# A decoder step for a prompt and eight sequences: the residual stream held feature-major, feed-forward unrolled in pairs

## The chip, the cores and the metric

One core of a Trainium2 chip runs the whole program. The metric is the device time of one execution in microseconds; the median of several runs is compared. In the profile the engines are PE (TensorE, with PEld for its weight loads), DVE (VectorE), ACT (ScalarE), POOL (GpSimd) and SP (SyncE, which here issues the transfers).

## The reference

One layer of a hybrid decoder is computed for 1024 prompt tokens and for 8 sequences of 4 new tokens: T = 1056 tokens in all, of D = 1024 features, which KD = 8 chunks of 128 partitions hold. All is fp32. Cut to what matters:

```python
def _rmsnorm(x, g):
    return x * rsqrt(mean(x * x, axis=-1) + NORM_EPS) * g

h = _rmsnorm(x, g_mix) @ w_in                     # split into u, v, q, k/v rows, gates
a_out = _gmlp_mixer(u, v)                         # causal gating in chunks of 128
b_out = nsa(q, ...)                               # compressed, selected and window branches, gated
x = x + concat(_rmsnorm(a_out, g_a), _rmsnorm(b_out, g_b)) @ w_o
mk, mv = _rmsnorm(mem, g_mem) @ w_mk, ... @ w_mv  # 256 memory tokens of the prompt
x = x + cross_attend(_rmsnorm(x, g_xa) @ w_xq, mk, mv) @ w_xo
a, g = h @ w_up, h @ w_gate                       # h = _rmsnorm(x, g_ffn), D_FF = 2816
x = x + (gelu(conv3(a) + conv_b) * g) @ w_down
y = _rmsnorm(x, g_final)
```

The samples take their past from a paged cache (gathered by a page table), from a window cache and from a cache of memory keys and values.

## The kernel before, in words

The program is a row of blocks, each with one hand-written stream for each engine, semaphores between the streams and a barrier at its end. A semaphore that an instruction waits for is named in the code (`pe.wait_ge(done, n)`). SP issues the loads in the order in which its stream has them, and a wait in that stream holds back all loads behind it.

*Layouts.* The residual stream `K.X` lies token-major: nine tiles of 128 tokens on the partitions (the last has the 32 sample rows), 1024 features in a row. Matmuls contract over the partitions, so what goes into a product as the normed input lies feature-major, `K.HT`: 8 chunks of 128 features, T = 1056 columns. A full fp32 product runs in two passes, and the trace has two records for it. In the feed-forward each operand is split into a high and a low part of type fp32r, and three products (high by high, high by low, low by high) take the place of the fp32 one.

*Norm of a tile* (`norm_phase`, and inside `project_norm`): ACT squares a row of 1024 with a running sum (L122), ACT takes the root (L127 or L343), DVE inverts and scales (L134, L141, L146), PE transposes the eight 128 x 128 blocks (L176, L298: a "turn"), DVE copies the result out times the gain (L156).

*The stages in order of time.* `norm_phase` "mix" with the bias rows (L1252, six small products of the relative bias table beside it); `feature_major` for w_in (L235: ring of two weight chunks, pieces of 352 columns, 8 chunks by 3 pieces by 8 products) while SP gathers pages of the cache (L460); gating (L538); compression; the samples' attention; the prompt's attention (L1080 to L1103); `project_norm` "wo" (L317, `w_o` as the moving operand in halves of 512 columns, token tile stationary, the norms of the two halves of the mix ahead of it and the next norm behind it, all by turns); norm "mem"; `feature_major` for w_mk; `memory_values` (L1286); `feature_major` for w_xq; cross attention of prompt and samples; `project_norm` "xo", which also splits its result into `ff_in_high` (ACT) and `ff_in_low` (POOL); `ffn`.

*The samples' attention* works on four sequences at a time ("half" 0 and 1). A sequence's 32 query rows are 32 stationary columns, so the four write the four groups of 32 partitions of one bank. `score(half)` has one sequence after the other: two products of 512 keys of the gathered pages (L862), two of 32 new keys (L863, L864), 512 window keys (L865), 63 compressed keys (L866). PV (L901) has 15 blocks for each sequence, again one sequence after the other. Score(1) reads the pages that SP gathers anew once score(0) has released them.

*`ffn`* goes over 22 chunks of 128 hidden features. For each, up and gate (L1654) are 3 pieces of 352 by 8 by 3 products each. Five turns of a hardware loop hold four chunks and then their part of down (L1667): four quarters of 256 output features, nine token tiles, activations stationary, w_down moving. Weights come by SP to `ff_weights` and `ff_down`, ACT makes the high part (L1684, L1690), POOL the low part (L1605, L1609). DVE does the convolution (L1762 to L1774) and adds the down products to x (L1785). Two chunks and the rest of down follow behind the loop, and the final norm by tiles (ACT L1734, DVE L1792).

## Time and profile before

| what | us |
|---|---|
| runs before, median of 3 (lowest, highest) | 2360.38 (2358.34, 2360.42) |
| the profiled execution | 2355.33 |
| its span | 2353.5 |
| PE busy | 2177.7 (93%), 11612 instructions |
| PEld busy | 1687.5 (72%) |
| DVE busy | 755.6 (32%) |
| ACT busy | 546.3 (23%) |
| POOL busy | 243.8 (10%) |

The span runs from the first to the last instruction of the profiled execution; its own time is 1.83 us more. Busy time overlaps between engines, and PEld lies beside PE. The page's line on transfers has 145.62 MB moved, mean 62 GB/s.

### The profile page before, as it was taken

To read this page: it belongs to the slowest core of one execution; us is meant where nothing else is said; L and a number is where in the kernel's file an instruction comes from. 1 tells how busy PE (TensorE), PEld (TensorE's weight loads), DVE (VectorE), ACT (ScalarE), POOL (GpSimd) and SP (SyncE) were. 2 spreads that over 40 slices of the span, in tenths; PEclk is the share of its full clock that TensorE was granted. 3 is DMA by queue.
4 is the path that set the end of the run, shared out by engine and by line. 5 is a ranking of instruction groups with operands and counts; after the bars stand their busy time and mean duration, and the time that the engine had idled before them with its cause. 6 is when DMAs were issued, how large, how long until landed. Compare 5 with 4: busy or idle time off the path is not lost. (4 is left out here: it accounts for less than half of the span.)

```text
span 2353.5 us, 29783 instructions
## 1 busy us (share of the span) xinstructions
PE 2177.7 (93%) x11612; PEld 1687.5 (72%) x11612; DVE 755.6 (32%) x1767; ACT 546.3 (23%) x1293; POOL 243.8 (10%) x122
## 2 busy tenths in 40 slices
PE   7989989679999997998997889899999999999997
PEld 4655557357677774546566634399999999999996
DVE  2002240335455453320003212235244342443425
ACT  3013220025455553211002101222021120211203
POOL 0000000000000000000000001223123231232311
PEclk9999999879899998999999999999999999999998
DMA  7230036330010002004102420011111010110102
GB/s 250 77 118 2 1 96 184 99 121 23 23 45 22 22 0 107 0 1 161 45 27 108 161 108 1 20 47 55 37 54 55 19 63 28 54 55 21 62 14 91
DMA packets 89308, 145.62 MB, mean 62 GB/s; under 512 B 41005, under 2 KB 63597, under 8 KB 86925
## 3 DMA queue, kind: packets, MB, share of 16 engines
q1 hardware_dynamic: 85118, 140.95, 17.9%
q10 hardware_dynamic: 4088, 3.17, 0.5%
q8 instruction: 82, 1.34, 0.2%
q14 instruction: 20, 0.16, 0.0%
HBM read 132.95 MB, written 14.26 MB: 63 GB/s over the span
## 5 line engine op out<-in xcount | busy, mean ns | idle before, releaser
L1654 PE MATMUL ps<-ff_in_high,ff_weights_high 128*128 128x352 f32 x1056 | 342.8, 325 | 13.2 <-issue 6.9
L1654 PE MATMUL ps<-ff_in_low,ff_weights_high 128*128 128x352 f32 x1056 | 340.1, 322 | 0.0
L1654 PE MATMUL ps<-ff_in_high,ff_weights_low 128*128 128x352 f32 x1056 | 339.9, 322 | 0.0
L317 PE MATMUL ps<-big 128*128 128x512 f32 (+1 forms) x576 | 252.9, 598 | 1.3 <-PEq L1449 1.3
L1667 PE MATMUL ps<-ff_down_high,ff_act_high 128*128 128x256 f32 x792 | 228.8, 289 | 9.4 <-POOL ff_act_low L1614 5.2
L235 PE MATMUL ps<-big,top 128*128 128x352 f32 x768 | 229.4, 462 | 2.9 <-ACTq L242 2.9
L1667 PE MATMUL ps<-ff_down_low,ff_act_high 128*128 128x256 f32 x792 | 226.1, 286 | 0.0
L1667 PE MATMUL ps<-ff_down_high,ff_act_low 128*128 128x256 f32 x792 | 226.0, 285 | 0.0
L1654 PEld LDWEIGHTS ps<-ff_in_high,ff_weights_high 128*128 128x128 f32 x1056 | 199.5, 189 | 14.1 <-issue 7.7
L235 PEld LDWEIGHTS ps<-big,top 128*128 128x128 f32 x768 | 146.6, 191 | 85.9 <-ACTq L242 4.2
L317 PEld LDWEIGHTS ps<-big 128*128 128x128 f32 (+1 forms) x576 | 104.2, 183 | 137.9 <-issue 137.7
L1654 PEld LDWEIGHTS ps<-ff_in_low,ff_weights_high 128*128 128x128 f32 x1056 | 199.8, 189 | 0.0
L1654 PEld LDWEIGHTS ps<-ff_in_high,ff_weights_low 128*128 128x128 f32 x1056 | 199.2, 189 | 0.0
L1103 PE MATMUL ps<-top,big 128*128 128x128 f32 (+1 forms) x1184 | 166.7, 289 | 13.2 <-ACT big L1205 7.2
L1103 PEld LDWEIGHTS ps<-top,big 128*128 128x128 f32 (+1 forms) x1184 | 145.6, 194 | 32.2 <-ACT big L1205 15.4
L538 PE MATMUL ps<-big 128*128 128x512 f32 (+3 forms) x432 | 160.5, 533 | 6.6 <-DVE top L571 6.6
L1667 PEld LDWEIGHTS ps<-ff_down_high,ff_act_high 128*128 128x128 f32 x792 | 153.8, 194 | 12.2 <-DVE x L1785 6.6
L1667 PEld LDWEIGHTS ps<-ff_down_low,ff_act_high 128*128 128x128 f32 x792 | 154.1, 195 | 0.0
L1667 PEld LDWEIGHTS ps<-ff_down_high,ff_act_low 128*128 128x128 f32 x792 | 154.0, 195 | 0.0
L1785 DVE TENSOR_TENSOR x<-ps,x 128x256 f32<-128x256 f32 (+1 forms) x216 | 91.1, 423 | 191.9 <-PE ps L1667 190.3
L538 PEld LDWEIGHTS ps<-big 128*128 128x128 f32 (+1 forms) x432 | 78.6, 183 | 87.5 <-issue 80.2
L1605 POOL TENSOR_TENSOR ff_weights_low<-ff_weights,ff_weights_high 128x1024 fp32r<-128x1024 f32 x44 | 105.6, 2400 | 308.8 <-ACT ff_weights_high L1684 308.8
(273 smaller groups left out, 2545.4 us busy)
## 6 DMA issues: line engine op xcount, KB each, us to landing
ff_weights<-in_w_up SPq DMA_DIRECT2D x22, 512.0 KB, 3.6
ff_weights<-in_w_gate SPq DMA_DIRECT2D x22, 512.0 KB, 4.1
ff_down<-in_w_down SPq DMA_DIRECT2D x20, 512.0 KB, 3.8
x<-in_x_prompt SPq DMA_DIRECT2D x16, 512.0 KB, 9.3
big<-bias_rows SPq DMA_DIRECT2D x8, 960.0 KB, 4.6
top<-in_mem_kt SPq DMA_DIRECT2D x7, 1024.0 KB, 11.0
big<-in_w_tm SPq DMA_DIRECT2D x8, 652.0 KB, 17.4
top<-in_mem_v SPq DMA_DIRECT2D x5, 1024.0 KB, 17.3
```

Of the source, the lines that this page charges most:

```text
L235: last = nc.tensor.matmul(K.bank[3 * u + s][:, 0:b - a], ring[:, u, k, :], src[:, k, a:b], start=k == 0, stop=k == KD - 1)
L317: last = nc.tensor.matmul(K.bank[2 * (t % 2) + h][:r, :], src[:, k, t * P:t * P + r], w[:, h, k, :], start=k == 0, stop=k == KD - 1)
L538: last = nc.tensor.matmul(K.bank[3 * (t % 2) + s][:r, 0:b - a], K.HT[:, k, t * P:t * P + r], w[:, k, a:b], start=k == 0, stop=k == KD - 1)
L1103: last = nc.tensor.matmul(K.bank[7][:, 0:P], pt[u % 2][:w, first + x, :], v, start=first + x == 0, stop=end and x == len(bl) - 1)
L1605: nc.gpsimd.tensor_tensor(w_low[:, s], landing[:, s], w_high[:, s], ALU.subtract).then_inc(low_done[s], 1)
L1654: last = nc.tensor.matmul(K.bank[3 * s + x][:, 0:b - a], w[:, s, k, :], h[:, k, a:b], start=k + n == 0, stop=k == KD - 1 and n == 2)
L1667: last = nc.tensor.matmul(K.bank[6 + n % 2][:, 0:256], a[:, k, t * P:(t + 1) * P], w[:, q % 2, k, :], start=k + m == 0, stop=k == chunks - ...
L1785: nc.vector.tensor_tensor(x, K.bank[6 + n % 2][:rows_of(t), 0:256], x, ALU.add).then_inc(down_taken, 1)
```

## The change

*Residual stream.* `K.XT` holds x as 8 chunks of 128 features by 1056 tokens. The input comes so from memory (`xt`, three pieces of 352 tokens for all features, `PIECES`), the output goes so, and the memory tokens too (`mem_t`). A new class `FeatureNorm` norms a piece: ACT squares two halves of four chunks, DVE adds up the chunks (three additions: 8 to 4, 4 to 2, 2 to 1), one product with a matrix of ones sums over partitions and spreads the sum to all of them (`spread`, L123), ACT takes the root, DVE inverts and multiplies eight chunks by gain and inverse. In the input phase there is no adding up: the product with ones runs over all eight chunks.

*Blocks.* `input_phase` takes the place of the constants' block, `norm_phase` "mix" and `feature_major`; the bias products (L272) stand between the chunks of that product. `mix_output` takes the place of `project_norm` "wo", norm "mem", and the products of w_mk, w_mv and w_xq. `cross_output` takes the place of `project_norm` "xo". In both, w_o and w_xo are stationary, 8 output chunks by 3 pieces by 8 products of 352 columns.

*Samples.* Score and PV have the kind (or block) as the outer loop and the sequence as the inner one.

*Feed-forward.* No hardware loop. Down runs for each pair of chunks: w_down stationary, 3 pieces by 8 output chunks by 6 products of 352 columns. The last pair's weights use the places of the up and gate weights. The final norm goes by pieces; POOL multiplies pieces 0 and 1 by the inverse, DVE piece 2.

```diff
+class FeatureNorm:
...
+    def add_up(self, dve, p):
+        a, b = self.pieces[p]
+        sq = self.sq[p % len(self.sq)]
+        dve.wait_ge(self.squared, 2 * p + 2)
+        for i in range(self.adds):
+            w = KD >> (i + 1)
...
+            add = self.nc.vector.tensor_tensor(sq[:, 0:w, 0:b - a], sq[:, 0:w, 0:b - a], sq[:, w:2 * w, 0:b - a], ALU.add)
...
+    def spread(self, pe, p):
...
+        n = KD >> self.adds
+        for c in range(n):
+            last = self.nc.tensor.matmul(self.bank[:, 0:b - a], self.K.ones[:, :], self.sq[p % len(self.sq)][:, c, 0:b - a],
+                                         start=c == 0, stop=c == n - 1)
+        last.then_inc(self.total, 1)
...
+def input_phase(nc, K, I, O):
...
+            for p, (a, b) in enumerate(PIECES):
+                sp.dma_start(K.XT[:, :, a:b], I["xt"][:, :, a:b]).then_inc(x_came[p], 16)
...
+            weights(2)
+            sp.wait_ge(norm.scaled, 3)
+            sp.wait_ge(came, 48)
+            gather(sp, K, 0, "cmp", 0, 2)
+            weights(3)
+            gather(sp, K, 0, "cmp", 2, 2)
...
-                for n in range(4):
-                    s = 4 * half + n
-                    rows = slice(32 * n, 32 * n + 32)
-                    for i in range(2):
-                        nc.tensor.matmul(K.bank[i][rows, :], qbd[:, s, :], KS[:, n * 1024 + 512 * i:n * 1024 + 512 * i + 512], start=True, stop=True)
...
+                for kind in range(6):
+                    for n in range(4):
+                        s = 4 * half + n
...
-                for n in range(4):
-                    s = 4 * half + n
-                    rows = slice(32 * n, 32 * n + 32)
-                    for i, (x, w) in enumerate(blocks):
+                for i, (x, w) in enumerate(blocks):
+                    for n in range(4):
+                        s = 4 * half + n
+                        rows = slice(32 * n, 32 * n + 32)
...
+def mix_output(nc, K, I, O, memt, mkt, mv):
...
+            sp.wait_ge(wo_done, n_wo)
+            for h in range(2):
+                sp.dma_start(w_mv[:, h], I["w_mv"][h]).then_inc(mv_came[h], 16)
+            for c in range(2, KD):
+                sp.wait_ge(mk_done, c - 1)
+                sp.dma_start(mk_ring[:, c % 2], I["w_mk"][c]).then_inc(mk_came[c % 2], 16)
...
+                    for k in range(KD):
+                        last = nc.tensor.matmul(K.bank[n % 4][:, 0:b - a], w[:, c, k, :], K.HT[:, k, a:b],
+                                                start=k == 0, stop=k == KD - 1)
+                    last.then_inc(wo_done, 1)
+                    if p < 2 and c in (1, 3, 5):
+                        turn(3 * p + 3 + c // 2)
...
+def cross_output(nc, K, I, w, w_came, high, low, sq, root, first_chunk):
...
+                norm.root(act, p)
+                act.wait_ge(norm.scaled, p + 1)
+                for h in range(2):
+                    nc.scalar.activation(high[:, 4 * h:4 * h + 4, a:b], sq[:, 4 * h:4 * h + 4, 0:b - a], ACT.Copy).then_inc(high_made, 1)
...
+            def down(g):
+                pe.wait_ge(act_low, 2 * g + 2)
+                pe.wait_ge(d_low_made, 2 * g + 2)
+                for p, (a, b) in enumerate(PIECES):
+                    for o in range(KD):
+                        n = g * TILE + p * KD + o
+                        if n >= 2:
+                            pe.wait_ge(down_taken, n - 1)
...
+                            for m, (w, x) in enumerate(((dh, a_high), (dl, a_high), (dh, a_low))):
+                                last = nc.tensor.matmul(K.bank[6 + n % 2][:, 0:b - a], w[:, at], x[:, c % SLOTS, a:b],
+                                                        start=e + m == 0, stop=e == 1 and m == 2)
...
+            up_and_gate(0)
+            up_and_gate(1)
+            for g in range(PAIRS - 1):
+                up_and_gate(2 * g + 2)
+                if g == PAIRS - 2:
+                    up_and_gate(2 * g + 3)
+                down(g)
+                if g < PAIRS - 2:
+                    up_and_gate(2 * g + 3)
+            down(PAIRS - 1)
+            norm.spread(pe, 2)
```

How the change moves instructions is shown at three places. The first is TensorE's order in `score(0)` of the samples, before (these five rows stand there four times, once for each sequence):

```order
L862 MATMUL ps<-x,big 32x512 x2
L863 MATMUL ps<-top,big 32x32
L864 MATMUL ps<-top,big 32x32
L865 MATMUL ps<-top,big 32x512
L866 MATMUL ps<-top,big 32x63
```

And with the change (the first row behind the scores is a transpose of the probabilities' first block):

```order
L697 MATMUL ps<-top,big 32x63 x4
L697 MATMUL ps<-top,big 32x32 x8
L697 MATMUL ps<-x,big 32x512 x8
L697 MATMUL ps<-top,big 32x512 x4
L706 MATMUL ps<-ident,big 63x128
```

The same 24 products stand in groups of one kind, and in each group four neighbours write four different groups of 32 rows of the bank.

The second is SP's order from the load of w_o to that of w_xq, before:

```order
L259 DMA big<-in_w_o 128x4096 x2
L1964 DMA top<-in_mem_prompt 128x1024 x2
L203 DMA top<-in_w_mk 128x1024 x2
L284 UNCONDITIONAL_BRANCH
L100 UNCONDITIONAL_BRANCH
L259 DMA big<-in_w_mv 128x4096 x2
L99 UNCONDITIONAL_BRANCH
L215 UNCONDITIONAL_BRANCH
L203 DMA top<-in_w_mk 128x1024 x6
L214 UNCONDITIONAL_BRANCH
L1272 UNCONDITIONAL_BRANCH
L203 DMA top<-in_w_xq 128x1024 x2
```

And with the change:

```order
L1083 DMA big<-in_w_o 128x1024 x8
L1084 DMA top<-in_mem_t 128x2048
L1086 DMA top<-in_w_mk 128x1024 x2
L1088 DMA top<-in_w_xq 128x1024 x2
L1091 DMA big<-in_w_mv 128x4096 x2
L1094 DMA top<-in_w_mk 128x1024 x6
L1096 DMA out_mem_k<-top 128x2048
L1098 DMA out_mem_v<-top 128x2x1024
L1102 DMA top<-in_w_xq 128x1024 x6
```

The two loads of w_mv still stand ahead of the last six of w_mk, but no memory norm lies between the end of w_o, which they wait for, and the products of w_mk. The first two chunks of w_xq have moved ahead of both.

The third is TensorE's order in the product of w_xo. Before it goes by token tiles, a turn of the tile before behind each:

```order
L317 MATMUL ps<-big 128x512 x32
L298 MATMUL ps<-ident,ff_scaled 128x128 x8
L317 MATMUL ps<-big 128x512 x16
L298 MATMUL ps<-ident,ff_scaled 128x128 x8
L317 MATMUL ps<-big 128x512 x16
```

And with the change, up to the block's end (`ones` is the matrix of ones, `ff_squares` the added squares of a piece):

```order
L1277 UNCONDITIONAL_BRANCH
L1287 MATMUL ps<-big 128x352 x96
L123 MATMUL ps<-ff_squares,ones 128x352
L1287 MATMUL ps<-big 128x352 x64
L123 MATMUL ps<-ff_squares,ones 128x352
L1287 MATMUL ps<-big 128x352 x32
L123 MATMUL ps<-ff_squares,ones 128x352
L1272 UNCONDITIONAL_BRANCH
```

Nine turns have become three single products; the last of them stands behind all products of the block.

## Rows read from the trace of the kernel before

**Rows 1.** Stretches: start:end, length; busy (count) of PE, PEld, DVE, ACT, POOL; PEclk, DMA, GB/s
```profile
0.00:33.11 33.11, 15.88 (x84) 9.84 (x85) 16.78 (x31) 16.89 (x29) 0.40 (x6) 1.00 0.87 326
33.11:148.70 115.59, 115.55 (x384) 73.76 (x384) 0.00 (x0) 8.23 (x21) 0.00 (x0) 0.99 0.29 78
415.97:424.63 8.66, 8.61 (x48) 2.86 (x48) 0.01 (x1) 0.00 (x0) 0.00 (x0) 1.00 1.03 252
442.28:451.10 8.82, 8.82 (x59) 3.69 (x59) 2.47 (x6) 0.00 (x0) 0.00 (x0) 0.97 0.00 0
481.02:497.40 16.38, 16.33 (x120) 12.59 (x120) 0.01 (x1) 0.00 (x0) 0.00 (x0) 0.92 0.00 1
918.68:1059.60 140.92, 138.70 (x417) 65.44 (x416) 44.10 (x87) 20.79 (x53) 0.00 (x0) 0.99 0.04 16
1059.60:1069.10 9.50, 3.57 (x17) 3.28 (x17) 4.78 (x10) 2.59 (x5) 0.00 (x0) 0.64 0.84 329
1069.10:1099.20 30.10, 28.68 (x128) 23.90 (x128) 0.00 (x0) 2.68 (x7) 0.00 (x0) 1.00 0.43 140
1129.56:1243.40 113.84, 113.84 (x384) 72.88 (x384) 0.00 (x0) 8.23 (x21) 0.00 (x0) 1.00 0.11 36
1384.89:1526.87 141.98, 133.47 (x361) 59.94 (x361) 30.77 (x54) 25.11 (x48) 25.07 (x20) 0.97 0.04 11
1526.87:2332.25 805.38, 792.41 (x5498) 790.19 (x5499) 313.79 (x493) 140.30 (x199) 213.91 (x93) 0.99 0.14 43
2332.25:2353.50 21.25, 10.45 (x48) 8.77 (x47) 15.53 (x27) 14.18 (x28) 0.00 (x0) 0.62 0.53 204
```

**Rows 2.** The chain that ended last, in the feed-forward: start, us, engine, what
```profile
1646.96 49.21 PE ps L1667 x408
1696.17 1.61 issue
1697.78 68.96 PE ps L1654 x432
...
2281.20 22.91 PE ps L1654 x144
...
2309.26 23.00 PE ps L1667 x168
```

**Rows 3.** Groups of instructions: xcount | busy, mean ns | idle before
```profile
L1605 POOL TENSOR_TENSOR ff_weights_low<-ff_weights,ff_weights_high 128x1024 fp32r<-128x1024 f32 x44 | 105.6, 2400 | 308.8 <-ACT ff_weights_high L1684 308.8
L1764 DVE SCALAR_TENSOR_TENSOR ff_conv<-ff_row,ff_small,ff_conv 128x1024 f32<-128x1024 f32 x22 | 28.3, 1284 | 0.8
L1252 PE MATMUL ps<-top,table 33*8 33x512 f32 (+1 forms) x12 | 5.7, 555 | 0.0
```

**Rows 4.** Timeline of PE in score(0): start, us, engine, line, operation
```profile
417.84 0.60 PE L865 MATMUL ps<-top,big 128*32 128x512 f32 x1
417.85 0.62 PE L862 MATMUL ps<-x,big 128*32 128x512 f32 x1
418.27 0.59 PE L865 MATMUL ps<-top,big 128*32 128x512 f32 x1
```

**Rows 5.** Timeline of DVE behind the first PV
```profile
465.05 0.29 DVE L927 COPY big<-ps 128x128 f32<-128x128 f32 x1 [10.21 <-PE ps L901]
```

**Rows 6.** Timeline of SP's queue, gather of the second half's pages
```profile
425.34 13.34 SPq L460 DMA_DIRECT2D big<-in_pool_sel  x16
```

**Rows 7.** DMA issues of 425 to 445: xcount, KB each, us from issue to landing
```profile
big<-in_pool_sel SPq DMA_DIRECT2D x16, 128.0 KB, 2.6
```

**Rows 8.** DMA issues of 1055 to 1100
```profile
big<-in_w_mv SPq DMA_DIRECT2D x2, 2048.0 KB, 9.6
```

**Rows 9.** Timeline of ACT, a square in the first norm
```profile
9.20 1.03 ACT L122 ACTIVATE ps<-x 128x1024 f32<-128x1024 f32 x1
```

**Rows 10.** Timeline of DVE and POOL in the feed-forward
```profile
2073.53 2.85 POOL L1609 TENSOR_TENSOR ff_down_low<-ff_down,ff_down_high 128x1024 fp32r<-128x1024 f32 x1
2074.04 2.37 DVE L1763 TENSOR_SCALAR ff_conv<-ff_row,ff_small 128x32 f32<-128x32 f32 x1
```

More of the change, by code:

```diff
@@ L129, in _, with square @@
-            if extra and "scalar" in extra:
-                extra["scalar"](act)
+            def square(p):
+                act.wait_ge(x_came[p], 16)
+                for h in range(2):
+                    norm.square(act, p, h)
+            square(0)
+            square(1)
+            act.wait_ge(eps_set, 1)
+            norm.root(act, 0)
+            square(2)
+            norm.root(act, 1)
+            norm.root(act, 2)
+            for n, (c, p) in enumerate(tiles):
+                a, b = PIECES[p]
+                act.wait_ge(done, n + 1)
+                nc.scalar.activation(K.FM[:, c, a:b], K.bank[3 * (c % 2) + p][:, 0:b - a], ACT.Copy).then_inc(taken, 1)
+                if c >= 2 and p == 2:
+                    x, y = cuts[c - 2]
+                    act.wait_ge(product, c - 1)
+                    nc.scalar.activation(vec[:, x:y], K.bank[7][:H, 0:y - x], ACT.Copy).then_inc(rows, 1)
@@ new lines, in _ @@
+            pe.wait_ge(ones_set, 1)
+            for p in range(3):
+                norm.spread(pe, p)
+            for n, (c, p) in enumerate(tiles):
+                a, b = PIECES[p]
+                if c < 2:
+                    pe.wait_ge(norm.scaled, p + 1)
+                else:
+                    pe.wait_ge(taken, nth[c - 2, p] + 1)
+                if p == 0:
+                    pe.wait_ge(w_came[c % 2], 16 * (c // 2 + 1))
+                for k in range(KD):
+                    last = nc.tensor.matmul(K.bank[3 * (c % 2) + p][:, 0:b - a], ring[:, c % 2, k, :], K.HT[:, k, a:b],
+                                            start=k == 0, stop=k == KD - 1)
+                last.then_inc(done, 1)
+                if c >= 2 and p == 2:
+                    x, y = cuts[c - 2]
+                    if c == 2:
+                        pe.wait_ge(came, 48)
+                    else:
+                        pe.wait_ge(rows, c - 2)
+                    nc.tensor.matmul(K.bank[7][:H, 0:y - x], K.table[:, :], oh[:, x:y], start=True, stop=True).then_inc(product, 1)
@@ new lines, in _ @@
+                nc.scalar.activation(a_high[:, c % SLOTS], ct, ACT.Copy).then_inc(act_split, 1)
+            for p, (a, b) in enumerate(PIECES):
+                for h in range(2):
+                    act.wait_ge(down_taken, LAST + KD * p + 4 * h + 4)
+                    norm.square(act, p, h)
+                act.wait_ge(norm.squared, 2 * p + 2)
+                for c in range(KD if p < 2 else TAIL, KD) if p == 2 else range(KD):
+                    last = nc.scalar.activation(K.XT[:, c, a:b], K.XT[:, c, a:b], ACT.Copy, scale=K.gains[:, 5, c:c + 1])
+                    if p == 2 and c == KD - 1 or p < 2 and c % 4 == 3:
+                        last.then_inc(gained, 1)
+                norm.root(act, p, free=(y, 2))
```

1132 lines of the change are left out of this document (525 added, 607 removed).

## The prediction

> **What bounds the kernel now.** I read the table of stretches first [rows 1]: TensorE is busy for all but a few tenths or a few microseconds of nearly every stretch, at a granted clock near 1.00. So the kernel is bound by TensorE's time in matmuls, and what the change can win is columns streamed, stretches in which small products could share the array, and the seams where TensorE stops. Then I read the chain of the feed-forward [rows 2]: it alternates 432 up and gate products (68.96 us, 0.1596 each) with 408 down products of 256 columns (49.21 us, 0.1206 each), and a return of the loop on TensorE of 1.6 to 1.8 us each time. Next came the mean durations of what will stand in the new seams [rows 3, 9], the TensorE timeline of the sample scores, and what surrounds them [rows 4 to 7]. The profiled execution took 2355.33 us, 1.83 more than its span and 5.05 less than the median of the runs (2360.38); I make the sum against the span and add both at the end. A measurement tells about 0.2% (4.7 us) of this kernel from no change.
>
> Two unit prices carry the sum. An fp32 product of 352 columns takes 113.84/192 = 0.593 us (two records each, [rows 1], the 1129.56 row). One of 512 columns is 0.863: the 918.68 row has 138.7 us busy in 417 records; 288 of them are 144 products, the others 16 turns (the eight transposes of a tile) of 0.9, which leaves 124.2.
>
> **The change part by part** (minus is faster).
>
> *Feed-forward, −42.4.* Before, 805.4 us = 22 chunks x 22.95 (68.96/3 and 22.91, [rows 2]) = 504.9; 2328 down products x 0.1206 = 280.8; five loop returns 8.5; a wait of 5.2 for the last activation, 2304.1 to 2309.3; 2.7 because the last 168 down products took 0.1369 instead of 0.1206; 3.3 start. After: down uses w_down as the stationary operand over 352 columns, 11 pairs x 144 products of the up form = 11 x 22.95, so 33 x 22.95 = 757.4, plus start 3.3 and 2.3 at the tail's edge: 763.0. Down alone goes from 2376 products (286.5 us, 48 of them in the tail's row) to 252.5: nine token tiles of 128 for 1056 tokens were 8% padding, which is 24 of these 34 us, and 352 columns cost 0.453 ns each for 0.471. The rest is the loop's seams and the last wait, which now has a whole down pair over it. A two-bank turn of down needs the DVE addition, 0.5 us, to come back in 0.96, so no stall; cost on SP, ACT, POOL stays hidden: they do the same splits, and the busiest of the splitting engines, POOL, has 213.9 of 805 [rows 1], 66 operations of 2.4 and 22 activations. If that cover fails, POOL's last difference of a chunk is late next, at 2.4 us a time, 53 over 22 chunks.
>
> *Sample attention, −26.* Four sequences write four column groups of 32. Score 0 takes 8.66 now; kinds outermost it is three groups of four 512-column products at 0.86 plus the small ones: 2.9. Score 1 then waits for the page gather: SP issues it from 425.34 for 13.34, landing 2.6 later, 441.3 [rows 6, 7], against 442.28 now, so only 1.0 comes of that. Score 1, 8.82, becomes about 4.6. VectorE's idle of 10.21 ahead of 465.05 was the first half's PV [rows 5], 16 us on TensorE like the second. With 1.0 from the gather, 4.2 from score 1 and 10.2 from this PV, what follows moves from 465.05 to about 449.7, −15.4. The second PV, 16.4 in 120 records, goes to 5.9: a quarter would be 4.1, strict order of records 8.2 to 9, and I take a little under the middle; −10.5. Together −26; −29 without lead times, −17 if pairs of records don't pack.
>
> The rows for this are the timeline's three [rows 4]: each fp32 product is two records. L862 of the next sequence starts at 417.85, beside the first record of L865 (417.84) and ahead of its second (418.27). So a product of another column group starts before the earlier one's second record, and four in a row should pack. The Trainium skill, in "TensorE: Matmul & The Clock Gate", section Part 3: Packing small matmuls — row/col tiling, says that matmuls are monotone in start and end in program order. By that rule this term would be −17 (rival 2); the trace speaks against applying it to the records of one product.
>
> *w_o to w_xq, −23.8.* The products: 192 x 0.593 = 113.9 for 124.2. Six turns of 0.93 remain inside the stretch (ten fewer, since the second norm is now a product with ones) = 5.6, and three spreads 1.5: 121.0 for 140.9, −19.9. Three turns ahead of the first product instead of two: +2.2. The memory norm's own block, 9.5 us with TensorE busy 3.57, disappears beside w_o: −9.5. w_mk: 28.7 of products, 0.6 of a spread, and a stall. SP issues both 2 MB halves of w_mv when w_o ends, ahead of w_mk's third chunk. The halves land after 9.6 in the median [rows 8], the second near 11, and 0.5 MB behind it at 329 GB/s is 13; it is needed at 7.3 (two chunks of 3.6), so 5.7, with 1.0 of start: +5.9 on 30.1. Ends: 0 if the queues interleave the loads, 10 if later chunks pay too. w_mv loses the block seam of 30.4 less 32 x 0.863: −2.5. w_xq is unchanged.
>
> *w_xo to the first feed-forward product, −3.6.* Before 142.0. After 113.9 + 1.2 of two spreads, then a tail that nothing covers: the last piece's addition 0.9, square of four rows 1.4 by [rows 9] (1.03 per 1024), additions 3.2, spread 1.2, root and reciprocal 1.0, eight scales 3.6 (1.284/1024 x 352 each, [rows 3]), high part 1.4, two POOL differences 6.6 (2.4/1024 x 1408 each), barrier 0.4, first weights 1.06 + 2.4: 23.3. Sum 138.4. Here the trace of before has no such tail; its bounds are −6 (high and low overlapped by halves) and +3 (VectorE stopped by POOL).
>
> *Input and feature-major product, +1.0.* The constants block goes, and x comes as three pieces of 1.44 MB; at 326 GB/s they land near 7, 11 and 15, squares 2.9 a piece, and the first product starts near 27 for 33.11: −6. Six bias products of 0.95 ([rows 3], 12 records) move from TensorE's idle time into the bound stretch: +5.5. SP's gathers stand between w_fm chunks, one of them late: +1.5. Bounds −5 and +6.
>
> *Final norm, −4.0.* 21.25 becomes 17.2: add 0.9, square 1.4, additions, spread and root 5.5, eight scales 3.6, output 3.0, and 2.8 for VectorE held by POOL's multiply of an earlier piece. The row for it: a 32-column VectorE operation took 2.37 us beside a POOL operation of 2.85 [rows 10], and 2.8 is taken for one such block. The Trainium skill, "SBUF — State Buffer", section Summary: rules for kernel authors, says that a VectorE operation with two SBUF inputs blocks fully until GpSimd's finishes; by that the tail would be 17.2, without it 14.4, and the trace agrees.
>
> *Cross attention, 0*: same instructions. **Sum**: −42.4 −26.0 −23.8 −3.6 +1.0 −4.0 = −98.8. Span 2254.7, profiled execution 2256.5, median of the runs 2261.5.
>
> **The rivals.**
> 1. *The forecast*, chance 0.60, 2261.5.
> 2. *Records start strictly in order.* A product's two records share a column group and follow each other, 0.43 apart. If the next group's first may not start before them, a round of four takes five such steps, 2.15 us, instead of two, 0.86. Score 0's share hides behind the gather; score 1 adds three rounds, 3.9, and each PV goes from 5.9 to 8.2 or more (15 rounds of five steps of 0.11): about 9 in all, 2270.5. Against it: [rows 4]. For it: only neighbours overlap today, 8.66 for a score whose twelve long products alone are 10.4 in a row. Chance 0.15.
> 3. *The new seams cost more*: w_mk pays for w_mv on each chunk (+4), late w_fm and 1408-byte rows of x (+5), VectorE blocked in both tails (+6): +15, 2276. For it: DMA bursts where weights are behind other loads, [rows 1], 1059.60 row. Chance 0.13.
> 4. *More gain*: the first product at 22 instead of 27, no w_mk stall, high and low overlapped: −14, 2247. Chance 0.10.
> 5. *The unrolled stream starves TensorE*, the case on the other side: the loop held 144-product pieces that ran again; now 4752 products with their weight loads are straight-line code, fetched once. The gain is gone at 98.8/4752 = 21 ns a product, 0.180 for 0.1596; at 30 ns the time is 2261.5 + 143 = 2404, slower. Against it: the 408 down products at 1646.96 [rows 2] are the loop's first pass, code not run before, and hold 0.1206. Chance 0.02.
>
> **How the numbers follow.** Rivals 2 to 4 lie at 2247, 2270.5, 2276; the forecast's own bounds (input ±5, w_xo ±5, w_mk ±5, sample +9/−3, tail ±2, drawn together some ±9) give 2252 to 2271. The range is 2245 to 2285: it takes in all three and leaves out the far ends of 3 and rival 5. Every case but the fifth is over 4.7 us faster, so faster 0.97, same 0.01, slower 0.02.
>
> **What would show it right or wrong.** In the feed-forward: no "issue" steps of 1.6 us in the chain, stretches of about 23 us for each of 33, the whole near 763; a mean product above 0.165 would be rival 5. In the sample stage: score stretches near 3 and 5 us and second PV near 6; if 5 and 9 or more, rival 2. w_mk: one wait on its DMA of about 6 us; the gap ahead of the feed-forward about 23; the first feature-major product at 27; the last product to the end 17. The forecast is wrong if the feed-forward is above 775, or the seams together miss by over 15.

## The result, and the profile after

The changed kernel takes 2281.61 us (median of 4 runs, 2280.03 to 2284.99) against 2360.4 for the one before (2358.34 to 2368.71): ratio 0.9662, interval 0.9636 to 0.9687, 78.8 us faster. Forecast were 98.8, and 2261.5 in a range of 2245 to 2285. The sign and the large parts came as forecast; the time is 20.1 above the forecast and near the range's upper end, because nearly every place where TensorE stops cost more than it was given.

The profiled execution took 2284.99 us with a span of 2283.0: 3.4 over the median of its runs, where that of before lay 5.05 below its own. So the two spans differ by 70.5 only, and 8.4 of the 28.3 that are missing between spans belong to these two executions and not to the change. The last section comes back to how executions of one kernel differ.

First the table of stretches of the changed kernel, in the order and with the columns of [rows 1]. Line by line: up to the first feature-major product, that product, score 0, score 1, second PV, w_o, w_mk, w_mv, w_xq, w_xo to the first feed-forward product, feed-forward to its last down product, and the rest:

```profile
0.00:31.46 31.46, 17.90 (x48) 10.72 (x49) 11.29 (x16) 11.49 (x10) 0.48 (x7) 0.95 0.95 344
31.46:154.54 123.08, 121.77 (x397) 73.77 (x395) 7.85 (x13) 14.63 (x30) 0.00 (x0) 0.99 0.27 73
417.07:420.09 3.02, 3.02 (x48) 0.91 (x48) 0.00 (x0) 0.00 (x0) 0.00 (x0) 1.00 1.18 298
444.50:448.81 4.31, 4.31 (x56) 1.56 (x60) 0.00 (x0) 0.00 (x0) 0.00 (x0) 0.69 0.00 0
468.96:475.41 6.45, 6.45 (x120) 4.88 (x120) 0.00 (x0) 0.00 (x0) 0.00 (x0) 0.57 0.01 3
899.92:1020.59 120.67, 120.67 (x439) 78.99 (x440) 49.03 (x86) 12.21 (x18) 0.00 (x0) 1.00 0.06 22
1020.59:1060.81 40.22, 32.01 (x132) 26.58 (x131) 9.97 (x13) 4.29 (x9) 0.00 (x0) 0.87 0.50 183
1060.81:1088.28 27.47, 27.47 (x66) 12.16 (x65) 0.00 (x0) 2.18 (x4) 0.00 (x0) 1.00 0.09 39
1088.28:1201.88 113.60, 113.60 (x384) 72.61 (x383) 0.00 (x0) 11.28 (x24) 0.00 (x0) 1.00 0.12 37
1341.83:1489.65 147.82, 118.08 (x390) 74.90 (x390) 40.41 (x60) 20.92 (x18) 21.19 (x8) 0.89 0.04 11
1489.65:2261.32 771.67, 763.61 (x4756) 761.45 (x4756) 329.46 (x534) 155.33 (x221) 219.55 (x90) 0.99 0.14 46
2261.32:2283.00 21.68, 1.54 (x2) 0.50 (x2) 14.35 (x15) 3.00 (x4) 7.65 (x2) 0.62 0.38 133
```

The products came as priced: 120.67 for w_o (forecast 121.0), 113.60 for w_xq (0.592 each), 27.47 for w_mv. Scores and PV packed: 3.02, 4.31 and 6.45 for 8.66, 8.82 and 16.38 (forecast 2.9, 4.6, 5.9). The second PV ran at a granted clock of 0.57, though; the first, the same 120 records, took 3.85 (from 448.63) at 1.00. What did not come is in rows with a gap between the length and PE's busy time: w_mk (40.22, of which 8.2 idle), w_xo (147.82, 29.7 idle), the feed-forward's end and the tail. From the last product to the end is 21.68, where the row of before shows 21.25 with products still in it. TensorE's idle time in the w_mk row is this wait (engine, line, what it waited for: us in total, times, longest):

```profile
PE ps L1237 <- DMA top<-in_w_mk: 8.2, 3, 7.5
```

The chain of the feed-forward, to be laid beside [rows 2] (start, us, what):

```profile
1489.65 71.51 PE ps L1678 x432
1561.17 22.89 PE ps L1695 x144
1584.05 45.79 PE ps L1678 x288
1629.84 22.89 PE ps L1695 x144
...
2204.10 31.19 PE ps L1695 x192
...
2247.89 4.58 DVE final_square L113
...
2261.92 0.97 DVE x L1806 x2
...
2264.32 2.30 DVE final_square L113
...
2266.64 3.73 DVE final_square L113
```

The 1.6 to 1.8 us of a loop's return are gone, and down is 22.89 a pair, 0.159 a product; 1584 such products take the place of 2376 of 0.1206. This price was read from the rows; no run changes the layout of down alone. Toward the end the chain leaves TensorE for VectorE's sums (L113).

Now the seam ahead of the feed-forward, after w_xo's last product (1458.36), from the timelines of DVE, ACT and POOL:

```profile
1458.40 0.53 DVE L1324 TENSOR_TENSOR x<-ps,x 128x352 f32<-128x352 f32 x1 [2.15 <-PE ps L1287]
1466.27 3.11 DVE L113 TENSOR_TENSOR ff_squares<-ff_squares 128x1408 f32<-128x1408 f32 x3 [7.34 <-ACT ff_squares L102]
1471.61 2.35 DVE L139 RECIPROCAL x<-x 128x352 f32<-128x352 f32 x1 [2.22 <-ACT x L132]
1474.00 4.06 DVE L146 SCALAR_TENSOR_TENSOR ff_squares<-x,gains 128x352 f32<-128x352 f32 x8
...
1463.60 2.64 ACT L102 ACTIVATE ff_squares<-x 128x1408 f32<-128x1408 f32 x2 [5.11 <-POOL ff_in_low L1313]
...
1457.30 6.26 POOL L1313 TENSOR_TENSOR ff_in_low<-ff_squares,ff_in_high 128x1408 fp32r<-128x1408 f32 x2 [32.17 <-ACT ff_in_high L1305]
1479.54 6.25 POOL L1313 TENSOR_TENSOR ff_in_low<-ff_squares,ff_in_high 128x1408 fp32r<-128x1408 f32 x2 [15.97 <-ACT ff_in_high L1305]
```

Two things were not in the forecast's 23.3: the squares of the last piece wait until POOL has made the low part of the piece before (1463.56), because both use the one buffer `ff_squares`; and the reciprocal of 352 columns takes 2.35.

### The profile page after: what moved, and what is told of

Same layout as the page of the kernel before. It is cut to its first block and busy times, and to the rows that moved or that the text cites. A ratio compares the mean times of both kernels' runs of the same rounds, so it can differ in the third digit from the quotient of the medians.

```text
span 2283.0 us, 27161 instructions
## 1 busy us (share of the span) xinstructions
PE 2086.4 (91%) x10848; PEld 1661.7 (73%) x10848; DVE 794.5 (35%) x1804; ACT 544.1 (24%) x1226; POOL 253.3 (11%) x110
## 5 line engine op out<-in xcount | busy, mean ns | idle before, releaser
L1806 DVE TENSOR_TENSOR x<-ps,x 128x352 f32<-128x352 f32 x264 | 138.2, 525 | 154.8 <-PE ps L1695 154.7
L1695 PE MATMUL ps<-ff_act_high,ff_down_high 128*128 128x352 f32 x480 | 154.9, 323 | 0.1
L1695 PE MATMUL ps<-ff_act_high,ff_down_low 128*128 128x352 f32 x480 | 153.8, 321 | 0.0
L1695 PE MATMUL ps<-ff_act_low,ff_down_high 128*128 128x352 f32 x480 | 153.8, 320 | 0.0
L371 PEld LDWEIGHTS ps<-big 128*128 128x128 f32 (+1 forms) x432 | 78.5, 183 | 86.7 <-issue 79.4
L1783 DVE TENSOR_SCALAR ff_conv<-ff_row,ff_small 128x1024 f32<-128x1024 f32 x22 | 38.5, 1752 | 250.9 <-ACT ff_row L1734 250.9
L1025 ACT ACTIVATE big<-big 128x63 f32<-128x63 f32 (+6 forms) x192 | 114.2, 597 | 38.5 <-DVE big L986 38.4
L1287 PE MATMUL ps<-big 128*128 128x352 f32 x384 | 115.7, 464 | 1.3 <-PEq L1484 1.3
L1219 PE MATMUL ps<-big 128*128 128x352 f32 x384 | 115.3, 460 | 0.8 <-DVE big L1162 0.8
L1037 ACT COPY big<-ps 128x512 f32<-128x512 f32 (+3 forms) x152 | 72.7, 536 | 154.0 <-PE ps L926 154.0
## 6 DMA issues: line engine op xcount, KB each, us to landing
top<-in_mem_kt SPq DMA_DIRECT2D x7, 1024.0 KB, 12.2
top<-in_mem_v SPq DMA_DIRECT2D x5, 1024.0 KB, 17.2
```

What stands on the lines that cost most here:

```text
L371: last = nc.tensor.matmul(K.bank[3 * (t % 2) + s][:r, 0:b - a], K.HT[:, k, t * P:t * P + r], w[:, k, a:b], start=k == 0, stop=k == KD - 1)
L1025: nc.scalar.activation(s[:, x:y], s[:, x:y], ACT.Exp, bias=m[:, 4 + b:5 + b], accum_out=m[:, 8 + b:9 + b]).then_inc(exps, 1)
L1037: last = nc.scalar.copy(pt[u % 2][:, x:x + len(full), :], K.bank[4 + b][:, 0:len(full) * P].rearrange("p (b n) -> p b n", n=P))
L1219: last = nc.tensor.matmul(K.bank[n % 4][:, 0:b - a], w[:, c, k, :], K.HT[:, k, a:b], start=k == 0, stop=k == KD - 1)
L1287: last = nc.tensor.matmul(K.bank[n % 4][:, 0:b - a], w[:, c, k, :], K.HT[:, k, a:b], start=k == 0, stop=k == KD - 1)
L1695: last = nc.tensor.matmul(K.bank[6 + n % 2][:, 0:b - a], w[:, at], x[:, c % SLOTS, a:b], start=e + m == 0, stop=e == 1 and m == 2)
```

## The experiments

Executions of the changed kernel lie up to 5 us apart, those of the kernel before up to 10. Where a variant has a single execution, the verdict is therefore taken from the stretch that the edit touches, and the whole time, given beside the changed kernel's median of 2281.6, tells little by itself. The stretches are steadier: the gap from w_xo's last product to the feed-forward, called the seam below, is 31.27 to 31.29 in the changed kernel and in all seven variants of it that leave it alone.

**The reciprocal.** VectorE's reciprocal gives way to a multiplication by 1.0, so the kernel leaves out the inverse of the root in its feature-major norms.

```diff
-        self.nc.vector.reciprocal(r, r).then_inc(self.rstd, 1)
+        self.nc.vector.tensor_scalar(r, r, 1.0, None, ALU.mult).then_inc(self.rstd, 1)
```

> The changed kernel with one edit: the reciprocal of 352 columns that every feature-major norm has on VectorE is replaced by a multiplication by 1.0 of the same shape, so the inverse of the root is left out of all norms but the two of the mix. Theory A: the misses in the seams come from this operation, 2.35 us where the forecast had 0.5. Then its time falls to about 0.5, the first feature-major product starts near 29.6 instead of 31.46, the gap ahead of the feed-forward falls from 31.3 to about 29.4, and the end moves by 2 to 4 more; in all 6 to 9 us less. Rival B: the misses are waits for POOL (its multiplication and its low parts), and the reciprocal stands beside them: the gap ahead of the feed-forward stays at 31 within 0.5 and the total falls by less than 3.

Measured: 2271.76, 9.8 less. The seam falls from 31.3 to 27.3, the tail (last product to the end) from 21.7 to 17.9. In VectorE's timeline of this run the operation takes 0.34:

```profile
1466.57 0.34 DVE L139 TENSOR_SCALAR x<-x 128x352 f32<-128x352 f32 x1 [2.22 <-ACT x L132]
```

Theory A holds for the two seams: 2.0 comes in each from the operation itself, and 2.0 more in the first since the piece before also comes to POOL earlier and frees the shared buffer earlier. In the tail 1.0 more comes since the reciprocal of the piece before no longer holds up the last two additions, and 0.7 since the last sums take 5.9 for 6.6. It does not hold for the first product, which did not move (31.7): there TensorE itself is the bound, see below.

**Two buffers of squares.** The second is the part of the normed input that w_xo's first piece has left.

```diff
-                if p:
-                    act.wait_ge(low_made, 2 * p)
+                if p > 1:
+                    act.wait_ge(low_made, 2 * p - 2)
...
+        sq = [norm_mem.enter_context(nc.sbuf_tensor("ff_squares", [P, KD, FREE3], F32)), K.HT[:, :, 0:FREE3]]
```

> The changed kernel with one edit: in the block of w_xo the squares have two buffers in turn (the second is the part of the normed input that the first piece has left), so that the square of the last piece does not wait for POOL's low part of the piece before. Theory: ScalarE's squares start about 0.5 to 1 after the last addition instead of 4.7 later, the gap ahead of the feed-forward falls from 31.3 to about 27, and the total by 4 to 5. Rival: VectorE's additions of the squares now run beside POOL's low part and are blocked by it, so that the gap falls by less than 2.

Measured: 2277.3, 4.3 less; the seam is 28.4, 2.8 less. Both theories have a part. Counted from w_xo's last product, the square starts 5.2 earlier, and then:

```profile
1457.28 5.48 DVE L113 TENSOR_TENSOR ff_squares<-ff_squares 128x1408 f32<-128x1408 f32 x3 [2.13 <-ACT ff_squares L102]
...
1453.52 6.27 POOL L1313 TENSOR_TENSOR ff_in_low<-big,ff_in_high 128x1408 fp32r<-128x1408 f32 x2 [32.15 <-ACT ff_in_high L1305]
```

The three additions take 5.48 beside POOL's operation, which ends at 1459.79, and 3.11 alone. So 2.4 of the 5.2 come back as blocking.

**POOL in the final norm.** VectorE multiplies pieces 0 and 1 by the inverse root, one half of piece 1 in the wait for the squares, one in the wait for root.

```diff
-                    nc.gpsimd.tensor_tensor(x, x, root[:, p % 2, :].unsqueeze(1).to_broadcast([P, 4, b - a]), ALU.mult).then_inc(y, 1)
+                nc.vector.tensor_tensor(x, x, root[:, p % 2, :].unsqueeze(1).to_broadcast([P, 4, b - a]), ALU.mult).then_inc(y, 1)
```

> The changed kernel with one edit: in the final norm VectorE, not POOL, multiplies pieces 0 and 1 by the inverse root. Theory: VectorE's sums of squares, 6.1 and 6.6 us beside POOL's multiplications, fall to 3.1 each although VectorE has 6 us more of its own; the waits of TensorE in the last pair fall by about 3 and the last product to the end from 21.7 to about 19; total 4 to 7 less. Rival: VectorE's own work simply takes the place of the blocking: total within 2 of the changed kernel.

Measured: 2281.48 in all, but 6.6 us of this run lie in the prompt's attention (410.3 for 403.7 in the others), which the edit does not touch. From the end of the last gate product to the end it is 73.6, for 80.9 in the changed kernel's profile and 79.3 to 80.5 in other runs; the tail alone is 18.5. So the theory holds in the stretch, and the rival's number in the whole time comes from elsewhere. The sums are back to 3.1 each:

```profile
2253.06 3.10 DVE L113 TENSOR_TENSOR final_square<-final_square 128x1408 f32<-128x1408 f32 x3
2264.24 3.10 DVE L113 TENSOR_TENSOR final_square<-final_square 128x1408 f32<-128x1408 f32 x3
```

**More banks for the last two pairs.**

```diff
+    MORE = {PAIRS - 2: (6, 7, 0, 1, 2), PAIRS - 1: (2, 3, 4, 5, 6, 7, 1)}
...
-                                last = nc.tensor.matmul(K.bank[6 + n % 2][:, 0:b - a], w[:, at], x[:, c % SLOTS, a:b],
+                                last = nc.tensor.matmul(bank_of(g, j)[:, 0:b - a], w[:, at], x[:, c % SLOTS, a:b],
```

> The changed kernel with one edit: the last two pairs of down use five and seven PSUM banks in turn instead of two, so that TensorE need not wait for VectorE's addition while VectorE does the convolution or the sums of the final norm. Theory: the wait of 1.9 at 2202 and those of about 7.5 in the last pair vanish, the feed-forward from its first product to its last falls from 771.7 to about 763; but the last addition waits for VectorE all the same, so the total falls by less, 3 to 6. Rival: VectorE is the bound of the last pair, the total falls by less than 2.

Measured: 2276.99, 4.6 less as a whole, but the last two pairs and the tail are 79.1, hardly under the other runs' 79.3 to 80.5. The waits tell why (engine, line, what it waited for: us in total, times, longest):

```profile
PE ps L123 <- DVE final_square L113: 7.9, 2, 6.2
```

The product with ones stands in TensorE's stream behind the fourth tile of the next piece and waits there for VectorE's blocked sums; banks for the tiles behind it don't help. The forecast 763 for the feed-forward was not reached (769.5), and the rival is nearer.

**Both, and that product two tiles later.** This run joins three changes: the banks, VectorE in POOL's place, and the product with ones two tiles later. In VectorE's stream the reciprocal of the piece before and its multiplications stand later, too, than in the run with VectorE alone.

```diff
-                        if g == PAIRS - 1 and p and o == 3:
+                        if g == PAIRS - 1 and p and o == 5:
                             norm.spread(pe, p - 1)
```

> The changed kernel with the last two pairs of down over five and seven banks, VectorE multiplying instead of POOL, and the product with ones placed two tiles later in TensorE's stream, so that it does not hold the stream while it waits for the sums. Theory: TensorE's place of waiting was that product, not the banks; with both the feed-forward from its first product to its last falls from 771 to about 763, and with the tail of 18.5 of the run with VectorE alone, the total is 9 to 11 under the changed kernel. Rival: VectorE's work is the bound of the last pair and the total is the 7 under it that VectorE alone gave.

Measured: 2269.42, 12.2 less. The stretch of the feed-forward and the tail:

```profile
1485.58:2245.63 760.05, 758.93 (x4756) 757.82 (x4756) 325.36 (x534) 155.17 (x221) 213.29 (x88) 1.00 0.13 45
2245.63:2267.40 21.77, 1.54 (x2) 0.50 (x2) 17.49 (x20) 3.00 (x4) 0.00 (x0) 0.61 0.56 199
```

760.05 for 771.67, with TensorE idle for 1.1: below the forecast's 763.0. In the two runs before it, TensorE waited 3.0 (VectorE alone) and 7.9 (banks alone) at the product with ones, here 1.1 inside the feed-forward. That fits its place in the stream as the cause, but no run moves that product alone, so how much each of the changes gives is not shown. The tail did not keep the 18.5 of the run with VectorE alone: it is 21.8, with VectorE busy for 17.5 of them, since multiplications of the first two pieces now stand in it. From the last gate product to the end it is 70.3, which is 3.3 under that run.

**w_mv behind w_mk.**

```diff
-            sp.wait_ge(wo_done, n_wo)
-            for h in range(2):
-                sp.dma_start(w_mv[:, h], I["w_mv"][h]).then_inc(mv_came[h], 16)
             for c in range(2, KD):
...
+            sp.wait_ge(wo_done, n_wo)
+            for h in range(2):
+                sp.dma_start(w_mv[:, h], I["w_mv"][h]).then_inc(mv_came[h], 16)
```

> The changed kernel with one edit: SP issues the two loads of w_mv behind the last chunk of w_mk instead of ahead of its third. Theory: the wait of w_mk's product for its third chunk, 7.5 us, falls to about 0 to 0.5 and no new one comes before w_mv, whose loads have 7 us of products left to hide under; the stretch of w_mk falls from 40.4 to about 32, total 7 to 8.5 less. Rival: the wait moves to w_mv, whose first half then lands late, and the total falls by less than 4.

Measured: 2270.87, 10.7 less as a whole. The two stretches, w_mk and w_mv, are 59.4 for 67.7, 8.3 less:

```profile
1015.92:1046.35 30.43, 29.02 (x131) 24.06 (x129) 9.97 (x13) 4.28 (x9) 0.00 (x0) 1.00 0.50 170
1046.35:1075.28 28.93, 27.74 (x66) 12.43 (x66) 0.00 (x0) 2.17 (x4) 0.00 (x0) 1.00 0.31 113
```

The wait of 7.5 is gone; w_mv waits 1.2 in its place. The w_mk row loses more than its wait, 9.8: in the changed kernel the 16 records behind the wait took 6.71, at a granted clock of 0.56 from 1035 to 1042, and here the same 16 take 3.72. So the wait cost 7.5 and 3.0 more in clock.

**The sequences one after the other.**

```diff
-                for kind in range(6):
-                    for n in range(4):
+                for n in range(4):
+                    for kind in (3, 4, 1, 2, 5, 0):
...
-                for i, (x, w) in enumerate(blocks):
-                    for n in range(4):
+                for n in range(4):
+                    for i, (x, w) in enumerate(blocks):
```

> The changed kernel with the samples' loops as they were before: one sequence after the other in score and PV. Theory: four neighbours that write four column groups run at the same time, and this alone gave what the sample stage gained: score(1) takes 8.8 instead of 4.3, the two PV 14 to 16 instead of 3.9 and 6.5, and the total rises by 22 to 26. Rival: the stage's gain came from the gather of the pages, which is issued at another time; then the total rises by less than 15.

Measured: 2307.45, 25.8 more; score 1 and the second PV are back:

```profile
444.40:452.80 8.40, 8.40 (x53) 3.16 (x54) 2.47 (x6) 0.00 (x0) 0.00 (x0) 0.96 0.00 0
483.23:499.61 16.38, 16.38 (x120) 12.63 (x120) 0.00 (x0) 0.00 (x0) 0.00 (x0) 0.91 0.00 1
```

The order of 168 small products alone is a third of the whole gain. Score 1 starts at 444.4 here and at 444.5 in the changed kernel, which waits 6.5 us for the pages first: faster scores before it gave nothing. As this run has the page gather of the changed kernel, the rival is refuted.

**The input block in another order.**

```diff
-            for p in range(3):
-                norm.spread(pe, p)
+            norm.spread(pe, 0)
+            norm.spread(pe, 1)
             for n, (c, p) in enumerate(tiles):
                 a, b = PIECES[p]
+                if n == 2:
+                    norm.spread(pe, 2)
...
-            gather(sp, K, 0, "cmp", 0, 2)
+            gather(sp, K, 0, "cmp", 0, 1)
```

> The changed kernel with one edit in two places of the input block: TensorE does the third spread only behind the first two tiles of the feature-major product, and SP gathers the pages in four parts between the weight chunks instead of two. Theory: the first product starts at about 26 instead of 31.5, the wait of 1.3 for a weight chunk goes, and the total falls by 5 to 7. Rival: a weight chunk behind a gather is late, the gain at the start comes back as a wait in the stretch, and the total falls by less than 2.

Measured: 2283.58, no gain, as the rival had it but by another way:

```profile
0.00:27.05 27.05, 12.66 (x33) 7.35 (x33) 6.47 (x10) 11.49 (x10) 0.48 (x7) 1.00 0.94 330
27.05:151.92 124.87, 124.87 (x412) 76.06 (x412) 12.67 (x18) 14.39 (x30) 0.00 (x0) 1.00 0.31 86
```

The product starts at 27.05, no weight is late, and it ends at 151.4 for 150.1 to 151.4 in other runs (the row has the last bias product, too): the moved product with ones costs its 4.9 us wherever it stands. TensorE was the bound there.

**So fewer of them.** With VectorE's sums ahead, three products with ones take the place of 24. The two edits of the run before stay in.

```diff
-    norm = FeatureNorm(nc, K, "mix", K.XT, K.gains[:, 0, :], PIECES, sq, root, K.bank[6], adds=0)
+    norm = FeatureNorm(nc, K, "mix", K.XT, K.gains[:, 0, :], PIECES, sq, root, K.bank[6])
```

> The changed kernel with one edit in the input block: VectorE adds up the chunks of the squares before the product with ones, as in the other norms (3 products instead of 24), the third spread behind two tiles, the gathers in four parts. Theory: TensorE is nearly the bound there from its first spread on, so 21 products of 352 columns, 12.6 us at full clock, are worth more than the place of a spread was; the first product starts at 24 to 25 instead of 30 and the product ends 4 to 5 earlier. Rival: VectorE, 9.5 us a piece, becomes the bound and the gain is under 2.

Measured: 2280.13, 1.5 less; the product starts at 24.5 and ends at 147.0, 3 to 4 earlier. The whole keeps nothing that can be told from noise: score 0 starts at 417.3 as it does at 417.07 in the changed kernel. Between them SP issues 64 page transfers, which start 2.8 earlier than in the run with the last pairs changed (341.4 for 344.2) and end no earlier (408.0 for 407.2).

**The low part by VectorE.**

```diff
-            for p, (a, b) in enumerate(PIECES):
+            for p, (a, b) in enumerate(PIECES[:2]):
                 for h in range(2):
                     pool.wait_ge(high_made, 2 * p + h + 1)
...
+                nc.vector.tensor_tensor(low[:, c, a:b], sq[:, c, 0:b - a], high[:, c, a:b], ALU.subtract).then_inc(low_made, 1)
```

> The changed kernel with one edit: the low part of the last piece in the block of w_xo is made by VectorE instead of POOL. Theory: 2 x 3.1 us on POOL become about 2 x 1.5 on VectorE, which is idle there: the gap ahead of the feed-forward falls from 31.3 to about 28, total about 3 less. Rival: a subtraction with two operands from SBUF and a rounded output takes VectorE as long as POOL, total within 1.

Measured: 2276.05, 5.6 less; the seam is 28.1, 3.2 less. One row has it, 3.16 for two operations that take POOL 6.25:

```profile
1475.37 3.16 DVE L1335 TENSOR_TENSOR ff_in_low<-ff_squares,ff_in_high 128x1408 fp32r<-128x1408 f32 x2 [1.44 <-ACT ff_in_high L1305]
```

**TensorE's loop written out in the kernel before.**

```diff
-            with pe.Fori(0, loops) as p:
+            for p in range(loops):
```

> The kernel before with one edit: TensorE's hardware loop in the feed-forward is written out (22 chunks and their down products in a straight line), the other engines keep their loops. Theory: straight-line products run at the same 0.1596 and 0.1206 us, and the five returns of TensorE's loop, 1.6 to 1.8 us each, go: 7 to 8.5 less unless another engine's return then ends last, in which case 3 to 7. Rival (the fifth of the prediction): fetching the written-out stream costs TensorE more, products get slower and the total rises.

Measured: 2348.8 (median of 5) against 2360.48, ratio 0.9956, interval 0.9939 to 0.9972: 10.4 less, 6.6 to 14.4. The chain of this run:

```profile
1662.42 49.22 PE ps L1667 x408
1711.64 68.70 PE ps L1654 x432
...
1806.24 49.22 PE ps L1667 x408
1855.46 68.70 PE ps L1654 x432
```

No issue step stands between down and up, one turn is 143.8 us for 145.65 before [rows 2], and 408 products take 49.22 as they did. The returns were worth their 8.5 (five turns by 1.83 are 9.2), and straight-line code costs TensorE nothing here.

**Together:** the loads of w_mv behind w_mk, the sums in the input block, two buffers of squares, the last pairs as above, and low parts 1 and 2 on VectorE, one of them in each of its two waits:

```diff
+            low_part(1, 0)
             norm.add_up(dve, 2)
+            low_part(1, 1)
             normed(2)
+            low_part(2, 0)
+            low_part(2, 1)
```

> The changed kernel with what the runs point to, together: w_mv's loads behind w_mk (-8.1 in its run), sums on VectorE in the input block (-3.4 at the end of that product, -1 in the whole run), two buffers of squares and the low parts of pieces 1 and 2 on VectorE in the block of w_xo (27.3 to 28.5 for 31.3 by one of them; both at once should leave 22 to 24), and the last pairs as in the run of that name (-12 against the usual 2279.4 of span). Theory: they stand in different places of the chain and add up: 8 + 1 to 3 + 8 + 12 = 29 to 31 us less, a median near 2251. Rival: the SP stream or the clock of TensorE after a gap takes part back; then 2256 to 2265.

Measured: 2254.58 (median of 5, 2252.94 to 2261.45) against 2359.03, ratio 0.9558, interval 0.9545 to 0.9571; 3.6 over what the parts add up to; where these 3.6 lie is open. It is 27 under the changed kernel's median and beats both kernels; the two were not timed in one comparison, but their intervals against the kernel before are apart. The seam is 22.9, inside the 22 to 24 expected, and the row from w_xo to the feed-forward is 140.94 for 147.82:

```profile
1335.75:1476.69 140.94, 119.60 (x391) 75.71 (x391) 46.60 (x64) 20.70 (x18) 8.71 (x4) 0.91 0.04 12
```

## Why the prediction was right, and where it was off

The forecast held in its sign and in its large terms: the unit prices of the products, the loop's returns, and the packing of the samples' products. It failed where TensorE waits. Its own sign for that was "the seams together miss by over 15", and this came true: 8.0 at the gap ahead of the feed-forward, 4.7 at the end, 4.5 at the first product (3 in most other runs) and 1.5 or more at w_mk's wait are over 18. The other sign, a feed-forward above 775, did not come. Of the gain, the order of the samples' products (25.8) and the loop's returns (about 10) were taken apart by runs; the rest is read from rows before and after.

- *Feed-forward, −42.4 forecast.* The unit price was right: 22.89 a stretch for 22.95. Measured between the profiles −33.7. Of the 8.7 missing, 2.0 is a wait at 2202 (VectorE has convolution and gate of the last chunk ahead of the additions) and most of the rest stands in the last pair, where TensorE's product with ones waits 6.4 in the stream for the sums of the norm. The step that failed is "a two-bank turn of down needs the DVE addition to come back in 0.96, so no stall": true for nine pairs, not for the last two, where VectorE has other work in between. With that out of the way the stretch is 760.05.
- *Sample attention, −26.* From the block's start to the prompt's attention 67.2 for 91.7: −24.5. The rows of before that spoke against rival 2 were right. Two sub-steps were wrong. The gather of the second half's pages does not wait for score 0 to release them, as the description of the kernel before and the forecast have it: it is issued from 409.97 before and from 412.34 now, ahead of score 0 in both, and [rows 6] shows its last 16 of 32 transfers only. Before, the pages were there when score 1 came behind its transposes; now score 1 waits 6.5 for them and starts 2.2 later, not 1.0 earlier. And PV was put at 5.9, "a little under the middle" between a quarter and strict order. At full clock it packs to 3.85, a quarter; that the second came to 6.45 is the clock of 0.57, so the nearness of 5.9 is luck.
- *w_o to w_xq, −23.8.* −20.2. The stall of w_mk was 7.5 and not 5.7, with 0.7 more at later chunks, and the lower clock behind it, 3.0, was in no term. For w_mv the forecast's own figures, 30.4 less 27.6, give −2.8 and not −2.5; measured is −2.9.
- *w_xo, −3.6.* +5.8, the largest miss for its size. The tail is 31.3 for 23.3: 4.7 the wait for POOL over the shared buffer, 1.9 root and reciprocal (2.9 for 1.0), 1.2 the second half of the square, 0.4 the scales. "Root and reciprocal 1.0" had no row behind it: the trace of before has reciprocals of one to three columns only, and the cost for each column had to be bounded and was not. The term's upper bound, +3, did not hold it.
- *Input, +1.0.* The first product came at 31.5 for 27 (29.9 to 30.4 in most other runs): three spreads of 16 records, which the forecast's 27 does not list, took 6.4, 6.7 and 5.0, and the later ones waited 2.8 for the root of the one before. The reciprocal does not show there, since without it the product started at 31.7. Six bias products cost 5.7 as priced. The block's product ends 5.3 later than in the profile of before, 1.4 to 2.7 in the other runs that don't touch it: within the bounds. When the samples' block starts, 2.6 of the 5.3 are left.
- *Final norm, −4.0.* +0.4: 21.7 for 17.2. The one block of 2.8 was 3.5, the reciprocal 1.85 more.
- *The rivals.* Rival 3 at 2276 (seams cost more) comes nearest, and with 0.13 it had too little. Its kind is right, its items only in part: VectorE is blocked by POOL at the end (3.5 for 2.8) and in the last pair, but w_mk paid once and not on each chunk, no w_fm chunk cost more than 1.3, and the seam ahead of the feed-forward had a shared buffer and a reciprocal that no rival names. Rival 4: the first product came later, not at 22, and w_mk did stall. Rival 2: refuted by 3.02 us for 48 records. Rival 5: refuted by 22.89 a stretch and by the written-out loop.

The prediction carried the 5.05 by which the profile of before lay under its median over to the changed kernel; had it not, its number would have been 25 off instead of 20.

## What to carry to other kernels

Turning a norm by tiles into one by pieces trades small, covered work on TensorE for a long chain over four engines at every seam: write that chain down operation by operation with the width each will have, and bound what the trace shows only narrow. A product that waits for another engine holds all products behind it, so place it in the stream where its operand is surely there. A wait of TensorE can cost more than its length, since the clock may be lower behind it: 3.0 on top of 7.5 here. Where an array's column groups are written by neighbours, put the neighbours next to each other in program order.

## What the runs showed of the hardware

**Reciprocal.** VectorE's reciprocal took 2.35 us for 352 columns, 6.7 ns a column, at all twelve places of that width; a multiplication by a constant of the same shape took 0.34, an addition from PSUM 0.53. At three columns it is 0.176, which shows nothing of this.

**Blocking.** Three additions of sums took 3.10 alone and 6.14 or 6.61 beside POOL's multiplication. The first of the three in the second norm started at 2247.81, 0.04 behind a POOL multiplication of 3.21, and ended 1.49 after it, 4.65 in all where 1.54 is usual. This is what the Trainium skill, "SBUF — State Buffer", section Summary: rules for kernel authors, says of a VectorE operation with two SBUF inputs that issues second beside a GpSimd operation that reads SBUF: it blocks fully until the first has finished. The run with VectorE in POOL's place, at 3.10, agrees. The row that the forecast took for it [rows 10] is of an operation with one tensor as input.

**Records of column groups.** Score 0 has 48 records, 12 long products of 0.86 and 12 short ones, in 3.02 us; in most other runs, where the granted clock was lower there (0.64), it took 4.6 to 4.7. Each pass of the four neighbours overlaps the others', so strict order by records, three rounds of 2.15 for the long ones alone, does not hold. The Trainium skill, in "TensorE: Matmul & The Clock Gate", section Part 3: Packing small matmuls — row/col tiling, says that matmuls start and end in program order. For the two records of an fp32 product this is not borne out: in [rows 4] the next sequence's first record, 417.85, starts ahead of the second record, 418.27, of the product before it.

**TensorE's clock in sparse stretches.** The profile of the unrolled kernel has the same first norm as the kernel before, and its first feature-major product starts at 41.14 instead of 33.11. TensorE waited 1.6 us for a transfer, and the granted clock of what followed was 0.55:

```profile
23.00:41.00 18.00, 17.03 (x52) 7.06 (x52) 9.19 (x16) 3.30 (x6) 0.00 (x0) 0.55 0.66 270
```

A turn took 1.97 there for 1.09, that is the lower of its two levels, 1.2 GHz. In the profile of before the clock stayed at 2.4 GHz. The same shows behind the wait of w_mk (granted clock 0.56, 16 records in 6.71 for 3.72) and in the second PV (0.57, 6.45 for 3.85). Between executions of one kernel the longer ones have the lower mean granted clock: the unrolled kernel took 2360.58 at 0.955 and 2345.60 to 2349.80 at 0.959 to 0.962, the kernel with everything together 2261.45 at 0.955 and 2252.94 to 2255.05 at 0.958 to 0.960. Of the difference in the unrolled kernel the start shown above has 8.0 us; that the clock explains the rest was not shown.
